# First block: mixer tokens in even, odd order, and two dilated head groups that score within one tile of 128 tokens

## The reference, cut to what matters

```python
ATTN_GROUPS = ((128, 1), (512, 4), (2048, 16))
def _dilated_group(q, k, v, bias, window, dilation):
    half = window // (2 * dilation)
    offs = dilation * np.arange(-half, half + 1)
    ...
        pos = q0 + t[:, None] + offs[None, :]
        valid = (pos >= 0) & (pos < S)
        logits = jnp.einsum('bqhd,bqkhd->bhqk', qb, kb) * scale
        logits = logits + bias.astype(jnp.float32)[None, :, None, :]
        logits = jnp.where(valid[None, None], logits, NEG_INF)
        lse = jax.nn.logsumexp(logits, axis=-1)
        p = jnp.exp(logits - lse[..., None]).astype(vb.dtype)
        o = jnp.einsum('bhqk,bqkhd->bqhd', p, vb)
...
    wts = jax.nn.softmax(jnp.stack(lses, axis=0), axis=0)
    attn = jnp.einsum('gbsh,gbshd->bshd', wts, jnp.stack(outs, axis=0).astype(jnp.float32))
```

## Time and profile before

| | us |
|---|---|
| median of 3 runs (1870.17 to 1871.05) | 1871.04 |
| the profiled execution's own time | 1866.34 |
| its span, first to last instruction | 1864.0 |
| PE busy | 1659.1 (89%) |
| PE weight loads busy | 1337.9 (72%) |
| DVE busy | 907.8 (49%) |
| ACT busy | 627.0 (34%) |
| POOL busy | 125.5 (7%) |
| bytes read from memory | 416.18 MB |

### The profile page before, as it was taken

One profiled execution on the slowest core, in us unless ns is written; L12 is line 12 of the kernel. 1 busy time (PEld: TensorE's weight loads), 2 busy tenths in 40 slices (PEclk: granted clock), 3 DMA queues, 4 the chain that ended last, 5 costly groups with the idle time before them and its releaser, 6 DMA issues.

```text
span 1864.0 us, 33345 instructions
## 1 busy us (share of the span) xinstructions
PE 1659.1 (89%) x14777; PEld 1337.9 (72%) x14777; DVE 907.8 (49%) x1227; ACT 627.0 (34%) x792; POOL 125.5 (7%) x103
## 2 busy tenths in 40 slices
PE   8999999999999999999989999989999757556575
PEld 7999998998799999899879896678864222212221
DVE  4445566664544466566565868887623111101111
ACT  4445444544334544454454222424313000000100
POOL 0600000000060000000003530000000000000000
PEclk9999999999999999999999999999999878878888
DMA  8652366754666336677433230000089999999997
GB/s 301 219 191 96 136 213 256 269 192 172 224 252 236 120 114 212 243 264 250 172 111 109 73 103 11 24 3 4 3 351 379 424 426 427 426 425 424 427 427 304
DMA packets 129489, 419.99 MB, mean 225 GB/s; under 512 B 14178, under 2 KB 35357, under 8 KB 109906
## 3 DMA queue, kind: packets, MB, share of 16 engines
q1 hardware_dynamic: 128930, 417.87, 58.9%
q10 hardware_dynamic: 432, 0.22, 0.0%
HBM read 416.18 MB, written 1.89 MB: 224 GB/s over the span
## 4 chain that ended last, share of the span: by engine, by line
PE 62%; DMA 16%; DVE 10%; ACT 5%; SPq 4%; issue 2%; DVEq 0%; ACTq 0%
PE bank L1295 32%; DMA R<-w_exp_down 15%; SPq L1190 4%; PE bank L1463 3%; PE ps_s L1409 3%; PE ps_t L1409 3%; ACT w_high L1933 2%; PE ps_t L1463 2%; PE bank L1481 2%; PE ps_s L1463 2%; DVE w_low L2388 1%; PE ps_s L1901 1%; PE ps_t L1481 1%; PE ps_t L1901 1%; PE ps_s L1481 1%
## 5 line engine op out<-in xcount | busy, mean ns | idle before, releaser
L2388 DVE TENSOR_TENSOR w_low<-wring,w_high 128x2048 fp32r<-128x2048 f32 (+1 forms) x127 | 287.0, 2260 | 302.6 <-ACT w_high L1933 302.2
L1933 ACT ACTIVATE w_high<-wring 128x2048 fp32r<-128x2048 f32 (+1 forms) x127 | 236.2, 1860 | 332.9 <-PE bank L1295 301.1
L1295 PE MATMUL bank<-x_high,w_high 128*128 128x256 f32 x1600 | 324.0, 284 | 7.7 <-DVEq L2439 7.7
L1295 PE MATMUL bank<-x_low,w_high 128*128 128x256 f32 x1600 | 320.0, 282 | 0.0
L1295 PE MATMUL bank<-x_high,w_low 128*128 128x256 f32 x1600 | 318.5, 280 | 0.0
L1295 PEld LDWEIGHTS bank<-x_high,w_high 128*128 128x128 f32 x1600 | 245.9, 190 | 14.6 <-DVEq L2439 8.7
L1295 PEld LDWEIGHTS bank<-x_high,w_low 128*128 128x128 f32 x1600 | 246.4, 189 | 0.0
L1295 PEld LDWEIGHTS bank<-x_low,w_high 128*128 128x128 f32 x1600 | 245.2, 189 | 0.0
L1883 PE MATMUL bank<-R 128*32 128x512 f32 x640 | 142.1, 716 | 107.9 <-DMA wring<-w_exp_up 70.9
L1883 PEld LDWEIGHTS bank<-R 128*32 128x32 f32 x640 | 35.5, 129 | 202.3 <-issue 125.1
L1883 PE MATMUL bank<-wring,R 128*32 128x512 f32 x384 | 141.8, 706 | 0.0
(11 more groups left out here) (690 smaller groups left out, 2984.5 us busy)
## 6 DMA issues: line engine op xcount, KB each, us to landing
wring<-w_in SPq DMA_DIRECT2D x29, 2048.0 KB, 8.2
R<-w_exp_up SPq DMA_DIRECT2D x24, 2048.0 KB, 37.1
R<-w_exp_down SPq DMA_DIRECT2D x24, 2048.0 KB, 43.5
wring<-w_up SPq DMA_DIRECT2D x22, 2048.0 KB, 8.6
R<-w_exp_gate SPq DMA_DIRECT2D x16, 2048.0 KB, 34.9
wring<-w_exp_gate SPq DMA_DIRECT2D x16, 2048.0 KB, 32.5
wring<-w_ada SPq DMA_DIRECT2D x12, 2048.0 KB, 10.1
wring<-w_down SPq DMA_DIRECT2D x10, 2048.0 KB, 7.9
```

Source lines behind the costliest of these rows:

```text
L1295: mm = pe.matmul(b[:, i * S:(i + 1) * S], left, right, start=k == 0 and m == 0 and i == 0, stop=k == last and m == 2, skip_group_check=True)
L1933: a.activation(high_of(l, job), half_block(l, job, wring), ACT.Copy).then_inc(w_high_ready, 1)
L2388: v.tensor_tensor(half_block(l, job, w_low), half_block(l, job, wring), high_of(l, job).bitcast(F32), ALU.subtract).then_inc(w_low_ready, 1)
```

## The change

For the mixer of the first block, tokens are kept in the order of all even ones, then all odd ones. `x_high` and `x_low` are written in that order from the banks of `x1`; the queries, keys and values follow from them. `u` is put back into its natural order when ACT empties its bank, POOL writes `poolT` in the new order, and the split of `mT` for `wo` returns to the natural order. In the new order a tile of 128 tokens is one parity, so the groups with even dilation have scores and value products within the tile only: 256 + 128 + 128 = 512 columns (`LW`) instead of 768, and 4 blocks of 128 (`PB`) instead of 6. The bias gets two layouts and two DMAs, and the addition of scale and bias becomes two instructions.

```diff
+PB = ST + NG - 1
+LW = PB * P
...
         bias = part(N_HEADS, 384)
+        bias_flat = bias[:, :, :].rearrange("p h j -> p (h j)")
+        n_all = HEADS_PER_GROUP * (S + 1)
+        bias_all = bias_flat[:, 0:n_all].rearrange("p (h j) -> p h j", j=S + 1)
+        bias_own = bias_flat[:, n_all:n_all + (N_HEADS - HEADS_PER_GROUP) * P].rearrange("p (h j) -> p h j", j=P)
...
+            if by_parity:
+                return x[:, 4 * hh:4 * hh + 4, :].rearrange("p k (c t n) -> p k t c n", c=2, t=ST)[:, :, t, :, :]
             return x[:, 4 * hh:4 * hh + 4, t * P:(t + 1) * P]
+        def half_bank(job, by_parity):
+            b = bank[JOB[job] % 4][:, :]
+            if by_parity:
+                return b.rearrange("p (k n c) -> p k c n", k=4, c=2)
+            return b.rearrange("p (k s) -> p k s", s=P)
+        def in_order(x):
+            return x.rearrange("p a (n c) -> p a c n", c=2)
+        def parity_order(x):
+            return x.rearrange("p a (c n) -> p a c n", c=2)
...
-                    sp.dma_start(bias[:, :, :], bass.AP(tensor=tab_dram.tensor, offset=0,
-                                                        ap=[[1, P], [512, N_HEADS], [1, 384]])).then_inc(hankel_in, 16)
+                    sp.dma_start(bias_all, bass.AP(tensor=tab_dram.tensor, offset=0,
+                                                   ap=[[2, P], [512, HEADS_PER_GROUP], [1, S + 1]])).then_inc(hankel_in, 16)
+                    sp.dma_start(bias_own, bass.AP(tensor=tab_dram.tensor, offset=512 * HEADS_PER_GROUP,
+                                                   ap=[[1, P], [512, N_HEADS - HEADS_PER_GROUP], [1, P]])).then_inc(hankel_in, 16)
...
-                        mm = pe.matmul(ps_s[:, g * S:(g + 1) * S], qT[:, hd, t * P:(t + 1) * P], kT[:, hd, :],
-                                       start=True, stop=True)
+                        o, keys = (0, kT[:, hd, :]) if g == 0 else (S + (g - 1) * P, kT[:, hd, t * P:(t + 1) * P])
+                        mm = pe.matmul(ps_s[:, o:o + keys.shape[1]], qT[:, hd, t * P:(t + 1) * P], keys, start=True, stop=True)
...
-                    for k in range(NG * ST):
+                    for k in range(PB):
...
-                            mm = pe.matmul(b[:, 0:S], vtok[:, t, hd * HD:(hd + 1) * HD], probT[:, hh % 2, g * ST + t, :],
-                                           start=g == 0 and t == 0, stop=g == NG - 1 and t == ST - 1)
+                            k, q = (t, slice(0, S)) if g == 0 else (ST + g - 1, slice(t * P, (t + 1) * P))
+                            mm = pe.matmul(b[:, q], vtok[:, t, hd * HD:(hd + 1) * HD], probT[:, hh % 2, k, q],
+                                           start=g == 0 and t == 0, stop=g == NG - 1, skip_group_check=True)
...
+                    a.activation(half_tile(j, x_high, name == "x1"), half_bank((name, j), name == "x1"), ACT.Copy).then_inc(x_high_ready, 1)
...
+                    if name == "u":
+                        a.activation(in_order(dst), b[:, :].rearrange("p (a c n) -> p a c n", a=2, c=2), func)\
...
-                    L = logit[:, i % 2, :]
+                    L = logit[:, i % 2, 0:LW]
...
+                    a.activation(in_order(x_high[:, 2 * j:2 * j + 2, :]), parity_order(mT[:, 2 * j:2 * j + 2, :]), ACT.Copy)\
...
+                    v.tensor_tensor(half_tile(j, x_low, name == "x1"), half_bank((name, j), name == "x1"),
+                                    half_tile(j, x_high, name == "x1").bitcast(F32), ALU.subtract).then_inc(x_low_ready, 1)
...
-                        L.rearrange("p (g s) -> p g s", s=S), ps_s[:, 0:NG * S].rearrange("p (g s) -> p g s", s=S),
-                        HD ** -0.5, bias[:, hh::HEADS_PER_GROUP, P * t:P * t + S][:, :, ::-1],
-                        ALU.mult, ALU.add).then_inc(logits_taken, 1)
+                        L[:, 0:S].rearrange("p (c n) -> p c n", c=2), ps_s[:, 0:S].rearrange("p (c n) -> p c n", c=2), HD ** -0.5,
+                        bias_all[:, hh, t:t + S][:, ::-1].rearrange("p (n c) -> p c n", c=2), ALU.mult, ALU.add)
+                    v.scalar_tensor_tensor(
+                        L[:, S:LW].rearrange("p (g s) -> p g s", s=P), ps_s[:, S:LW].rearrange("p (g s) -> p g s", s=P),
+                        HD ** -0.5, bias_own[:, hh::HEADS_PER_GROUP, :][:, :, ::-1], ALU.mult, ALU.add).then_inc(logits_taken, 1)
...
+                                  ps_t[:, 0:LW].rearrange("p (k q) -> p k q", q=P)).then_inc(probT_ready, 1)
...
+                    v.tensor_tensor(in_order(x_low[:, 2 * j:2 * j + 2, :]), parity_order(mT[:, 2 * j:2 * j + 2, :]),
+                                    in_order(x_high[:, 2 * j:2 * j + 2, :]).bitcast(F32), ALU.subtract).then_inc(m_low_ready, 1)
...
+                    ins = g_eng.tensor_tensor(parity_order(poolT[:, 2 * g:2 * g + 2, :]), in_order(dst[:, :, 0:S]),
+                                              in_order(u[:, :, PAD:PAD + S]), ALU.subtract)
```

More of the change, by code:

```diff
@@ L32 @@
 N_HEADS = HEADS_PER_GROUP * NG
+assert all(dilation % 2 == 0 for _, dilation in GROUPS[1:])
+PB = ST + NG - 1
+LW = PB * P
 HD = 128
@@ L147, in first_constants @@
     hot = np.zeros((N_BUCKETS + 1, NG, 512), np.float32)
-    d = np.arange(S - 1, -S, -1)
     for g, (window, dilation) in enumerate(GROUPS):
+        d = np.arange(S - 1, -S, -1) if g == 0 else 2 * np.arange(P - 1, -P, -1)
         half = window // (2 * dilation)
@@ L154, in first_constants @@
             hot[bucket.get(x, N_BUCKETS), g, i] = 1.0
-        hot[N_BUCKETS, g, 2 * S - 1] = 1.0
+        hot[N_BUCKETS, g, len(d):] = 1.0
     inv = np.zeros((len(POOL_WINDOWS), S), np.float32)
@@ L529, in build @@
         bias = part(N_HEADS, 384)
+        bias_flat = bias[:, :, :].rearrange("p h j -> p (h j)")
+        n_all = HEADS_PER_GROUP * (S + 1)
+        bias_all = bias_flat[:, 0:n_all].rearrange("p (h j) -> p h j", j=S + 1)
+        bias_own = bias_flat[:, n_all:n_all + (N_HEADS - HEADS_PER_GROUP) * P].rearrange("p (h j) -> p h j", j=P)
         upad = part(KT, UW)
         probs_at = at[0]
-        probT = part(2, NG * ST, S)
+        probT = part(2, NG * ST, S)[:, :, 0:PB, :]
         inv = part(len(POOL_WINDOWS), S)
@@ L1961, in turned @@
                     wait_full(a, l, (name, j))
-                    a.activation(half_tile(j, x_high), bank[JOB[(name, j)] % 4][:, :].rearrange("p (k s) -> p k s", s=P),
-                                 ACT.Copy).then_inc(x_high_ready, 1)
+                    a.activation(half_tile(j, x_high, name == "x1"), half_bank((name, j), name == "x1"), ACT.Copy).then_inc(x_high_ready, 1)
             for l in range(DEPTH):
@@ L1968, in evac @@
                     b = bank[JOB[(name, j)] % 4]
+                    if name == "u":
+                        a.activation(in_order(dst), b[:, :].rearrange("p (a c n) -> p a c n", a=2, c=2), func)\
+                            .then_inc(act_emptied, 1)
+                        return
                     a.activation(dst, b[:, 0:n] if len(dst.shape) == 2 else
@@ L2044, in _ @@
                     a.wait_ge(m_ready, 4 * l + j + 1)
-                    a.activation(x_high[:, 2 * j:2 * j + 2, :], mT[:, 2 * j:2 * j + 2, :], ACT.Copy).then_inc(m_high_ready, 1)
+                    a.activation(in_order(x_high[:, 2 * j:2 * j + 2, :]), parity_order(mT[:, 2 * j:2 * j + 2, :]), ACT.Copy)\
+                        .then_inc(m_high_ready, 1)
                 high(l, SPLIT[("wb", 3)] + 2)
@@ L2434, in turned @@
                     v.wait_ge(x_high_ready, 4 * (2 * l + n) + j + 1)
-                    v.tensor_tensor(half_tile(j, x_low), bank[JOB[(name, j)] % 4][:, :].rearrange("p (k s) -> p k s", s=P),
-                                    half_tile(j, x_high).bitcast(F32), ALU.subtract).then_inc(x_low_ready, 1)
+                    v.tensor_tensor(half_tile(j, x_low, name == "x1"), half_bank((name, j), name == "x1"),
+                                    half_tile(j, x_high, name == "x1").bitcast(F32), ALU.subtract).then_inc(x_low_ready, 1)
                 v.wait_ge(x_low_ready, 4 * (2 * l + n) + 4)
@@ L2460, in _ @@
                 if l == 0:
-                    v.wait_ge(hankel_in, 16)
+                    v.wait_ge(hankel_in, 32)
                 v.wait_ge(pooled, l + 1)
@@ L2491, in take_probT @@
                     v.tensor_copy(probT[:, hh % 2, :, t * P:(t + 1) * P],
-                                  ps_t[:, 0:NG * S].rearrange("p (k q) -> p k q", q=P)).then_inc(probT_ready, 1)
+                                  ps_t[:, 0:LW].rearrange("p (k q) -> p k q", q=P)).then_inc(probT_ready, 1)
                 def pv_low(hh):
@@ L2530, in m_low @@
                     v.wait_ge(m_high_ready, 4 * l + j + 1)
-                    v.tensor_tensor(x_low[:, 2 * j:2 * j + 2, :], mT[:, 2 * j:2 * j + 2, :], x_high[:, 2 * j:2 * j + 2, :].bitcast(F32),
-                                    ALU.subtract).then_inc(m_low_ready, 1)
+                    v.tensor_tensor(in_order(x_low[:, 2 * j:2 * j + 2, :]), parity_order(mT[:, 2 * j:2 * j + 2, :]),
```

(1 more changed line is left out.)

4 lines of the change are left out of this document (1 added, 3 removed).

## The result

| | before | after |
|---|---|---|
| median of the runs taken together | 1870.61 us (1869.45 to 1871.05, 4 runs) | 1851.26 us (1849.41 to 1852.84, 4 runs) |
| ratio to before | | 0.9893, 95% interval 0.988 to 0.9906 |
| the profiled execution's own time | 1866.34 | 1849.41 |
| its span | 1864.0 | 1847.4 |
| PE busy | 1659.1 | 1642.3 |

The change is faster by 19.4 us on the medians and by 16.6 us between the two profiled spans.

A forecast was written before the change was run, and what follows sets the result against it. Two chains of nearly equal length, PE's and the ACT/DVE loop's, were taken to bound the gate stage. Per layer 5.5 + 2.6 = 8.1 us, two layers 16.2 us, so 1871.0 - 16.2 = 1854.8 us; range 1852 to 1863.5.

The forecast's parts named there:

- The loop up to `scores(7)`: Gate stage, ACT/DVE loop from first exponential to scale-and-bias of `logits(6)`: narrower operations bring `scores(7)` 5.5 us earlier per layer.
- The pair of 256: Scale and bias as two 256-column instructions in the gate stage: 0.78 us per step instead of 0.98, gaining 0.20 each.
- From `scores(7)` to `wa`: End of the gate stage, where PE is the path: narrower scores, transposes, copy and value products save 2.6 us per layer.
- Strides at nothing: Stride-2 reads and writes at `x1`, `mT`, the bias, `u` and POOL's subtraction: taken to cost zero.
- the PSUM rule: PSUM lines hold 8 bytes, so non-contiguous patterns slow matmuls; if ACT's and DVE's reads too, 2.2 us per layer at `x1`.
- 1: Strided PSUM reads cost double, 2.2 us per layer at `x1`: 1859.2 us, or 1863.4 with bias and `mT` doubled; chance 0.17.
- 4: Strided elements take three or more times as long at `x1`, `mT` and bias: slower, 1879 us; chance 0.04.
- 2: Narrow f32 matmuls in the gate stage get no cheaper: only 2.3 us gained per layer, 1866.4 us; chance 0.04.
- 3: The gain is lost at the next weight wait, for `w_up`, which grows by 8 us: 1871 us; chance 0.05.
- the sum: Both layers' gate stages: 8.1 us each, 16.2 us in all, subtracted from the whole kernel's median of 1871.0.
- moved or added elsewhere: Outside the gate stage: two bias DMAs, strided POOL and ACT work, `x1` and `mT` accesses; all taken to cost nothing.
- PE's arrival: PE stands ready for `scores(7)` at 199.8, the loop 0.3 us later; allows at most 0.3 us more gain per layer.

The follow-up runs named there:

- the two half changes: Kernel before with only PE's attention work narrowed, 1862.82 us; kernel before with only the ACT/DVE logits, maximum and softmax narrowed to 512 columns, 1868.27 us.
- natural_order: The changed kernel with every token reordering and strided access taken out, so two head groups see wrong keys; 1849.74 us.
- after_again: The changed kernel itself, run once more for its spread and a second trace; 1849.47 us.
- after_64_nops: The changed kernel with 64 empty PE instructions added at its start; 1852.38 us.

## Why the prediction was right, and where it failed

- **What bounds the kernel: right.** Two chains of nearly equal length in the gate stage. Shown by the two half changes: 1.35 and 0.6 us a layer alone, 7.95 together.
- **The loop up to `scores(7)`, 5.5 us: right within 0.3.** `scores(7)` came 5.4 us earlier (205.62 to 200.25), of which 0.1 lies ahead of the stage. The pair of 256, taken at 0.76 from rows of another operation, took 0.42 + 0.34.
- **From `scores(7)` to `wa`, 2.6 us: 2.8 measured.**
- **Strides at nothing: right within 0.1 us a layer**, by 2.50 beside 2.41 us and by `natural_order`. With it the PSUM rule of the Trainium skill (SBUF — State Buffer, Door 1: The DMA port swizzle) does not carry over to the reads by ACT and DVE here: these have stride 2 in f32 and cost 0.1 us in 2.5. Whether it holds for matmuls no run here shows.
- **Rivals.** 1 and 4 fall by those same numbers, 2 by 1.14 us for `scores` (1.56 before) and 3 by the unchanged 7.69 us.
- **The step that failed is the sum.** "Per layer 5.5 + 2.6 = 8.1 us; two layers 16.2 us" was 15.9 and held, but it was taken for the whole. The part on what is "moved or added elsewhere" has no term for the 32 transposes that go out of PE's stream: they take the 2.0 us stall ahead of the experts with them, 600 us after the last edited line. Nothing in the diff points there; the row "issue" among PE's waits in the second block of before did, and the prediction reads PE's waits in the gate stage alone.
- **The stall alone does not carry the time out of the range.** 15.9 + 2.0 = 17.9 us is what the traces account for, and 1870.6 - 17.9 = 1852.7. The median lies 1.4 us below that, and 0.4 us of the miss is the median of before, taken at 1871.0 and now 1870.6. Against its own group's median of before, the same remainder is 3.8 us in `after_again`, 3.5 in `natural_order` and -0.1 in `after_64_nops`, so it is no fixed term. The interval of the first comparison, 17.6 to 22.4 us, holds 17.9; that of `after_again`, 19.1 to 24.7, does not.
- **Where the remainder lies.** In each pair of traces it lies in stages with a different time at half clock: the first spans differ by 16.6 us and the second by 22.6. The largest place is the stretch from 902.51 to 1181.44 us of before. It took 278.9 and 278.8 us in the two traces of before and 276.6 and 276.5 in the two of after, but 278.2 in `after_64_nops`. The mean clock of a run does not tell: in the three groups, the 17 runs of before at 0.950 took from 1866.9 to 1874.5 us with a median of 1870.0, and the three of `after_again` at 0.950 took 1849.1 to 1849.9, which is 20 us less. Whether the change moves the falls of the clock to cheaper places or this is luck isn't shown.
- **The low end of the range had no room.** For more gain than forecast the prediction names only PE's arrival, 0.3 us a layer, and 1852 lies 2.8 us below the forecast. With 2.0 us for stalls elsewhere it would have been 1850, which holds 1851.3 and not the 1849.5 of `after_again`; that takes some 2 us for the clock besides.

## What to carry to other kernels

Where an order of queues closes a loop beside a busy engine, work out both chains and shorten both; one alone gave a thirteenth to a sixth of the gain here. A change that removes or adds instructions on an engine moves every later instruction in its stream, so list the "issue" waits of the whole program before costing the edit, and leave room for them at both ends. Compare two traces of one program before explaining a difference of a few us between two programs, and compare them by stage, with the granted clock beside each.

## What the runs showed of the hardware that was not expected

- PE stalls for 1.2 to 2.0 us at a fixed place in its instruction stream, behind 12462 matmul records in six traces of five kernels, where that place lies in a burst of small matmuls. In the seven traces in which it lies among matmuls of 0.43 us, one step in one trace is 0.14 us longer and nothing else shows. PE goes on 1.23 to 1.43 us after the end of a 16 KB packet of the instruction queue.
- Empty instructions did not move that place: 64 and 192 of them left no record.
- A wait of 1.8 us behind sparse transposes is followed by some 3.4 us at half clock in some runs and not in others; one filler matmul of 0.85 us in it was enough, in the one trace that tried it. Each such fall costs 1.5 us in matmul-bound work, yet removing three of them did not shorten the whole. Near the end of the program, a last fall of 6.8 us instead of 3.4 costs 1.35 us.
